# A hybrid decoder step: the recurrence entered out of the last attention step, its inputs read back in five batches, and the output norm and gate taken by thirds of the tokens over four row strips

## What is computed

```python
x = x + 0.5 * swiglu(rms_norm(x, ffn1_norm), ffn1_up, ffn1_down)
z_rw, q, k, v, gates = split(rms_norm(x, mix_norm) @ w_in)
y_a, wkv, z_new = rwkv7_branch(z_rw, z_last, wkv0)     # the recurrence
o = attend(rope(q), rope(k), v)                        # two softmax maps per head, p1 - lam * p2
y_b = rms_norm(o, da_subln) * (1.0 - lam_init)         # over the 128 values of each of 4 heads
merged = sigmoid(gates_a) * (y_a @ w_proj_a) + sigmoid(gates_b) * (y_b @ w_proj_b)
x = x + merged @ w_out
x = x + 0.5 * swiglu(rms_norm(x, ffn2_norm), ffn2_up, ffn2_down)
# the end of rwkv7_branch, y from the scan over the tokens, 8 heads of 64:
y = (y - mean(y)) * rsqrt(var(y) + RW_GN_EPS)
y = y * rw_ln_w + rw_ln_b + sum(r * k * rw_r_k) * v
y = y * g                                              # g = sigmoid(gd) @ rw_g2
```

## Time and profile before

| | us |
|---|---|
| time, median of 3 runs | 2895.99 (2893.55 to 2904.36) |
| profiled execution, its own time | 2896.66 |
| its span, first to last instruction | 2895.0 |
| PE busy in it | 2737.5 (95%) |
| DVE busy | 1376.1 (48%) |
| ACT busy | 655.8 (23%) |

### The profile page before, as it was taken

How to read it: one execution, slowest core, us unless ns; L and a number is a source line. 1 busy time by engine, 2 the same in 40 slices (tenths; PEclk the granted TensorE clock), 3 DMA queues, 4 the chain that set the end, 5 groups by cost and what they waited for, 6 DMA issues and landing times.

```text
span 2895.0 us, 51864 instructions
## 1 busy us (share of the span) xinstructions
PE 2737.5 (95%) x21419; PEld 2578.9 (89%) x21419; DVE 1376.1 (48%) x1452; ACT 655.8 (23%) x969; POOL 267.7 (9%) x258
## 2 busy tenths in 40 slices
PE   6999999999999999997777899899999999999998
PEld 6999999999999999995343789759999999999998
DVE  4332233223574688667663687655443322332333
ACT  5111111111311222332332233212222111110223
POOL 1000000000001233102000555200000000000000
PEclk8999999999999999997988899969999999999999
DMA  3111111111323455569645000124211111111112
GB/s 103 44 51 51 44 43 47 48 49 40 112 87 103 154 170 188 190 191 344 202 126 152 27 26 25 32 89 132 78 47 43 50 45 51 43 50 45 44 42 75
DMA packets 270206, 252.12 MB, mean 87 GB/s; under 512 B 20724, under 2 KB 216144, under 8 KB 269920
## 3 DMA queue, kind: packets, MB, share of 16 engines
q1 hardware_dynamic: 252960, 189.42, 21.9%
q0 software_dynamic: 16896, 60.40, 5.7%
q10 hardware_dynamic: 192, 0.07, 0.0%
HBM read 209.93 MB, written 39.90 MB: 86 GB/s over the span
## 4 chain that ended last, share of the span: by engine, by line
PE 87%; DVE 7%; ACT 2%; issue 1%; SPq 1%; DMA 1%; DVEq 0%; POOL 0%; POOLq 0%; ACTq 0%
PE ps L1746 72%; PE ps L2060 1%; DVE small L1469 1%; PE ps L2080 1%; PE ps L2075 1%; PE ps L1790 1%; PE ps L2263 1%; PE ps L1976 1%; PE ps L1910 1%; DMA value_ring<-in_cache_v 1%; PE ps L2107 1%; PE ps L1994 1%; PE ps L1953 1%; PE ps L2115 1%; PE ps L2087 1%
## 5 line engine op out<-in xcount | busy, mean ns | idle before, releaser
L1746 PE MATMUL ps<-h_hi,w_hi 128*128 128x344 f32 x3072 | 991.8, 323 | 10.3 <-DVE w_lo L1188 10.3
L1746 PE MATMUL ps<-h_lo,w_hi 128*128 128x344 f32 x3072 | 980.6, 319 | 0.0
L1746 PE MATMUL ps<-h_hi,w_lo 128*128 128x344 f32 x3072 | 980.1, 319 | 0.0
L1746 PEld LDWEIGHTS ps<-h_hi,w_hi 128*128 128x128 f32 x3072 | 577.7, 188 | 25.9 <-issue 19.8
L1746 PEld LDWEIGHTS ps<-h_lo,w_hi 128*128 128x128 f32 x3072 | 578.0, 188 | 2.1 <-issue 1.9
L1746 PEld LDWEIGHTS ps<-h_hi,w_lo 128*128 128x128 f32 x3072 | 577.9, 188 | 0.0
L1746 PE MATMUL ps<-ff_hi,w_hi 128*128 128x344 f32 x1056 | 337.1, 319 | 0.0
L1746 PE MATMUL ps<-ff_lo,w_hi 128*128 128x344 f32 x1056 | 336.6, 319 | 0.0
L1746 PE MATMUL ps<-ff_hi,w_lo 128*128 128x344 f32 x1056 | 336.2, 318 | 0.0
L831 ACT ACTIVATE w_hi<-w_stage 128x1024 fp32r<-128x1024 f32 x194 | 203.8, 1051 | 479.8 <-PE ps L1746 479.8
L1188 DVE TENSOR_TENSOR w_lo<-w_stage,w_hi 128x1024 fp32r<-128x1024 f32 x194 | 239.2, 1233 | 139.1 <-ACT w_hi L831 103.8
(11 more groups left out here) (402 smaller groups left out, 3233.7 us busy)
## 6 DMA issues: line engine op xcount, KB each, us to landing
w_stage<-in_ffn_up SPq DMA_DIRECT2D x176, 256.0 KB, 3.1
key_ring<-in_cache_k SPq DMA_DIRECT2D x128, 256.0 KB, 2.9
value_ring<-in_cache_v SPq DMA_DIRECT2D x128, 256.0 KB, 3.0
w_stage<-in_w_in SPq DMA_DIRECT2D x84, 256.0 KB, 3.3
w_stage<-in_ffn_down SPq DMA_DIRECT2D x80, 256.0 KB, 2.9
gate_save<-tmp POOLq DMA_DIRECT2D x16, 516.0 KB, 4.5
gate_ring<-gate_save POOLq DMA_DIRECT2D x16, 516.0 KB, 4.3
row_ring<-row_save SPq DMA_DIRECT2D x40, 128.0 KB, 2.9
```

Of the source, the lines that this page charges most:

```text
L1746: last = mm(dense[s][:, j], w[w0][:, k0 + k, :], r[:, k, j * CH:(j + 1) * CH], start=(k == 0 and n == 0), stop=(k == nk - 1 and n == 2))
```

## The change

It does six things.

1. The groups of cached values are used in steps 4 to 29 in place of 4 to 31; steps 17, 19, 22, 25, 26 and 28 take two.
2. POOL's queue reads the recurrence's inputs back in five batches of four DMAs, each behind a wait for scores 10, 13, 16, 19 and 22.
3. The squares for the head norm are taken from each step's 128x128 output in bank 6 by ACT, straight behind the copy into `Q`. PE sums them in the next step (`square_sum`, one output row at partition 32 * head). ACT copies four rows at a time into `rmix`, and DVE adds and inverts them block by block (`o_inverse`).
4. `decays(0)` moves into step 30 on ACT. POOL's `gram_sides(0)` waits for the last transposes but one and for the last value group, no longer for the head norm's sums. PE's `blocks(0)` follows the last output's copy and square.
5. In the first chunk DVE inverts 136 columns where it inverted 1032.
6. The output norm and gate run by thirds of the tokens (344 columns): each of 12 parts makes four matmuls, one per head, from rows 0, 32, 64 and 96 into four banks, and DVE works on the four heads of a third. The order is bonus, root, gate, then the head norm's scale.

The core of the diff (the table of semaphores, tile places and two memsets left out):

```diff
-        FILL_STEP = [s for s in range(HP, STEPS) for _ in range(2 if s >= STEPS - HP else 1)]
+        FILL_STEP = [s for s in range(HP, STEPS - 2) for _ in range(2 if s in (17, 19, 22, 25, 26, 28) else 1)]
...
-            for dst, src, done in ((KKn, kk_save, "kk_back"), (Bf, b_save, "b_back"), (Kf, kp_save, "kp_back"),
-                                   (Rf, r_save, "r_back"), (Vf, v_save, "v_back")):
+            for dst, src, done, step in ((KKn, kk_save, "kk_back", 10), (Bf, b_save, "b_back", 13), (Kf, kp_save, "kp_back", 16),
+                                         (Rf, r_save, "r_back", 19), (Vf, v_save, "v_back", 22)):
+                pool.wait_ge(*ev.at("scores_done", step))
...
-            pool.wait_ge(*ev.at("o_sums", 1))
+            pool.wait_ge(*ev.at("w_trans_lo", STEPS - 1))
+            pool.wait_ge(*ev.at("w_trans_hi", STEPS - 1 - 4 * HP))
+            pool.wait_ge(*ev.at("value_used", 4 * NS))
...
+                if step == STEPS - 2:
+                    act.wait_ge(*ev.at("cum_back0", 16))
+                    act.wait_ge(*ev.at("gate_saved0", 8 * GT))
+                    act.wait_ge(*ev.at("gate_saved1", 8 * GT))
+                    decays(0)
                 act.wait_ge(*ev.at("o_done", step + 1))
-                sc.activation(Q[:, step % HP, qi * P:(qi + 1) * P], PS[:, 6, 0:P], ACT.Copy)\
-                    .then_inc(ev["o_moved"], 1)
+                sc.activation(Q[:, step % HP, qi * P:(qi + 1) * P], PS[:, 6, 0:P], ACT.Copy)
+                if step and step % HP == 0:
+                    sc.activation(rmix[:, (qi - 1) * P:qi * P], PS[:, 6, P:2 * P], ACT.Copy, scale=1.0 / P).then_inc(ev["o_rows"], 1)
+                if step == STEPS - 1:
+                    sc.activation(rmix[0:96, qi * P:NP], PS[0:96, 6, P:2 * P], ACT.Copy, scale=1.0 / P)
+                sc.activation(osq, PS[:, 6, 0:P], ACT.Square).then_inc(ev["o_moved"], 1)
...
-            act.wait_ge(*ev.at("o_sample", NS))
-            for h in range(HP):
-                sc.activation(osq[:, h, :], Q[:, h, :], ACT.Square).then_inc(ev["o_sq"], 1)
-            act.wait_ge(*ev.at("o_mean", 1))
-            sc.activation(rmix[0:HP], rmix[0:HP], ACT.Sqrt).then_inc(ev["o_root"], 1)
-            act.wait_ge(*ev.at("cum_back0", 16))
-            act.wait_ge(*ev.at("gate_saved0", 8 * GT))
-            act.wait_ge(*ev.at("gate_saved1", 8 * GT))
...
+            act.wait_ge(*ev.at("o_sample", NS))
+            sc.activation(osq_sample, Q[:, :, NP:NT], ACT.Square).then_inc(ev["o_sq"], 1)
             decays(1)
+            act.wait_ge(*ev.at("o_sums", 1))
+            sc.activation(rmix[96:P, NP - P:NP], PS[96:P, 3, 0:P], ACT.Copy, scale=1.0 / P)
+            sc.activation(rmix[:, NP:NT], PS[:, 3, P:P + NS], ACT.Copy, scale=1.0 / P).then_inc(ev["o_rows"], 1)
...
+            def o_inverse(qi):
+
+                b = slice(qi * P, (qi + 1) * P if qi < 7 else NT)
+                dve.wait_ge(*ev.at("o_rows", qi + 1))
+                in_turn(v.tensor_scalar(rmix[:, b], rmix[:, b], 0.0, EPS, ALU.max, ALU.add))
+                in_turn(v.reciprocal(rmix[:, b], rmix[:, b]).then_inc(ev["o_inverse"], 1))
...
+                if qi and step % HP == 1:
+                    o_inverse(qi - 1)
...
-                    dve.wait_ge(*ev.at("o_root", 1))
-                    in_turn(v.reciprocal(rmix[0:HP], rmix[0:HP]).then_inc(ev["o_rstd"], 1))
+                    o_inverse(7)
...
+            def square_sum(step, bank, at):
+
+                row = 32 * (step % HP)
+                return mm(PS[row:row + 1, bank, at:at + P], K("ones")[:, 0:1], osq, start=True, stop=True)
...
+                    square_sum(step - 1, 6, P)
...
-            turn_sums(NS - 1)
-
-            pe.wait_ge(*ev.at("o_sample", NS))
-            for h in range(HP):
-                pe.wait_ge(*ev.at("o_sq", h + 1))
-                for j in range(NCH):
-                    last = mm(dense[0][0:HP, j], osel[:, HP * h:HP * h + HP], osq[:, h, j * CH:(j + 1) * CH],
-                              start=(h == 0), stop=(h == HP - 1))
-            last.then_inc(ev["o_sums"], 1)
-            pe.wait_ge(*ev.at("o_mean", 1))
...
+            pe.wait_ge(*ev.at("o_moved", STEPS))
             blocks(0)
+            square_sum(STEPS - 1, 3, 0)
+            pe.wait_ge(*ev.at("o_sq", 1))
+            for h in range(HP):
+                last = mm(PS[32 * h:32 * h + 1, 3, P:P + NS], K("ones")[:, 0:1], osq_sample[:, h, :], start=True, stop=True)
+            last.then_inc(ev["o_sums"], 1)
...
-                in_turn(v.scalar_tensor_tensor(ch3(y), ch3(y), param("rw_ln_w", h), dense[part % 2], ALU.mult, ALU.mult)
-                        .then_inc(ev["y_used"], 1))
-                dve.wait_ge(*ev.at("y_parts", part + 2))
-                in_turn(v.tensor_tensor(ch3(t1), ch3(Vf[:, h, :]), dense[(part + 1) % 2], ALU.mult).then_inc(ev["y_used"], 1))
-                in_turn(v.scalar_tensor_tensor(y, y, param("rw_ln_b", h), t1, ALU.add, ALU.add))
-                if h:
-                    ya_low(h - 1)
-                dve.wait_ge(*ev.at("y_parts", part + 3))
-                in_turn(v.tensor_tensor(ch3(y), ch3(y), dense[part % 2], ALU.mult).then_inc(ev["y_used"], 1))
...
+                b, bonus = third_of(j), spread_at(j)
+                in_turn(v.tensor_tensor(ybonus[:, :, b], Vf[:, :, b], bonus, ALU.mult).then_inc(ev["y_used"], 1))
+            for j in range(NCH):
+                b, root = third_of(j), spread_at(NCH + j)
+                for h in range(HP - 1):
+                    in_turn(v.scalar_tensor_tensor(CUM[:, h, b], CUM[:, h, b], param("rw_ln_w", h), root[:, h], ALU.mult, ALU.mult))
+                in_turn(v.scalar_tensor_tensor(CUM[:, HP - 1, b], CUM[:, HP - 1, b], param("rw_ln_w", HP - 1), root[:, HP - 1],
+                                               ALU.mult, ALU.mult).then_inc(ev["y_used"], 1))
+                in_turn(v.tensor_tensor(CUM[:, :, b], CUM[:, :, b], ybonus[:, :, b], ALU.add))
+            for j in range(NCH):
+                b, gate = third_of(j), spread_at(2 * NCH + j)
+                for h in range(HP - 1):
+                    in_turn(v.scalar_tensor_tensor(CUM[:, h, b], CUM[:, h, b], param("rw_ln_b", h), gate[:, h], ALU.add, ALU.mult))
+                in_turn(v.scalar_tensor_tensor(CUM[:, HP - 1, b], CUM[:, HP - 1, b], param("rw_ln_b", HP - 1), gate[:, HP - 1],
+                                               ALU.add, ALU.mult).then_inc(ev["y_used"], 1))
+                if j:
+                    ya_low(j - 1)
+            for j in range(NCH):
+                b, scale = third_of(j), spread_at(3 * NCH + j)
+                for h in range(HP - 1):
+                    in_turn(v.scalar_tensor_tensor(ybonus[:, h, b], Q[:, h, b], param("da_subln", h), scale[:, h], ALU.mult, ALU.mult))
+                in_turn(v.scalar_tensor_tensor(ybonus[:, HP - 1, b], Q[:, HP - 1, b], param("da_subln", HP - 1), scale[:, HP - 1],
+                                               ALU.mult, ALU.mult).then_inc(ev["yb_full"], 1))
+                if j == 0:
+                    ya_low(NCH - 1)
+                else:
+                    yb_low(j - 1)
+            yb_low(NCH - 1)
...
-            for part in range(3 * HP):
-                h, kind = divmod(part, 3)
-                if part >= 2:
+            pe.wait_ge(*ev.at("ck_rows_in", NC))
+            for part in range(4 * NCH):
+                kind, j = divmod(part, NCH)
+                first, b = part % 2 * HP, third_of(j)
+                if part == 1:
+                    pe.wait_ge(*ev.at("wkv_made", 1))
+                if 2 <= part < 3 * NCH + 2:
                     pe.wait_ge(*ev.at("y_used", part - 1))
-                if part == 0:
+                if part == NCH:
                     pe.wait_ge(*ev.at("y_root", 1))
-                if part == 2:
+                if part == 2 * NCH:
                     pe.wait_ge(*ev.at("g2_loaded", 16))
                     pe.wait_ge(*ev.at("gd_back", 16))
-                q = slice(32 * h, 32 * h + 2)
-                for j in range(NCH):
-                    cols = slice(j * CH, (j + 1) * CH)
-                    if kind < 2:
-                        last = mm(dense[part % 2][:, j], K("row_heads")[q], Rf[q, kind, cols], start=True, stop=True)
-                    else:
-                        last = mm(dense[part % 2][:, j], G2[:, h * P:(h + 1) * P], gd[:, cols], start=True, stop=True)
+                if part == 3 * NCH:
+                    pe.wait_ge(*ev.at("o_root", 1))
+                if part == 4 * NCH - 1:
+                    pe.wait_ge(*ev.at("yb_full", 1))
+                for h in range(HP):
+                    out, q = PS[:, first + h, 0:CH], slice(32 * h, 32 * h + 2)
+                    if kind == 0:
+                        last = mm(out, K("row_heads")[q], Rf[q, 1, b], start=True, stop=True)
+                    if kind == 1:
+                        last = mm(out, K("row_heads")[q], Rf[q, 0, b], start=True, stop=True)
+                    if kind == 2:
```

(3 more changed lines are left out.)

120 lines of the change are left out of this document (55 added, 65 removed).

## The result

The changed kernel takes 2882.72 us (median of 13 runs, 2874.29 to 2886.55), the kernel before 2895.99 beside it (13 runs, 2891.59 to 2904.36): a ratio of 0.994, with a 95% interval of 0.993 to 0.995. It is faster by 0.6%. 1.5% was forecast, and 2882.72 lies above the range of 2843 to 2867. The profiled execution is the fastest of the 13: own time 2874.29, span 2872.5. The 13 fall into two groups, six from 2874.29 to 2878.65 and seven from 2882.72 to 2886.55; only one of the lower group was profiled, so what the upper group pays in addition isn't shown.

A forecast was written before the change was run, and what follows sets the result against it. Prediction: PE bounds the kernel, held back at the attention's exit, first chunk, and norm and gate. 2896.66 - 28.4 - 5.5 - 14.2 + 5 = 2853.6 us, forecast as 2853.5 (-1.5% against the median), range 2843 to 2867.

The forecast's parts named there:

- term 4: Attention: added squares, doubled value groups and late reloads cost +6.5 us summed, taken as +5, bounds -2 to +15.
- Late reloads: Attention, in term 4: three batches fall in waiting steps, each late by perhaps 1.2 us; first groups save 1: +2.5.
- each batch costs what its DMAs take in steps that wait, 3 x 5: Attention, upper bound of term 4: +15 us, with the rest cancelling.
- Later ones have most of a step in hand: Attention, in term 4: steps from 16 on have slack for late groups, so only three batches cost time.
- The clock: Attention, in term 4: PE's clock level was allowed 1 us each way.
- Term 1: Recurrence's start: `blocks(0)` can start 3.1 us after the last output's start in place of 31.6, gain 28.4 us.
- Term 2: First chunk: DVE's 6.59 us inversion becomes an addition and inversion of 136 columns, gain 5.5 us, between 3.5 and 7.
- Term 3: Norm and gate: four strips run side by side, DVE becomes the bound at 42.6 us; gain 14.2 us, bounds 11 to 16.
- Term 4 without the reloads: Attention: squares, doubled groups, `o_inverse` and shorter late steps, the +5 or +6.5 us less 2.5 for reloads.
- the attention pays much more: Rival, attention: batches stretch groups in flight, doubled steps run out of pages, 13 us plus 3 for squares; 2865 to 2874, chance 0.16.
- the stretches that were put at nothing: Before the first output product, the recurrence after its first chunk, and merge to the end: forecast difference 0.

The follow-up runs named there:

- early_again: The changed kernel with its twenty reload transfers issued together ahead of the attention, measured a second time: 2859.00 us, ratio 0.9869 to the kernel before.
- before_late: The kernel before with only the reloads changed, to five batches behind scores 10, 13, 16, 19 and 22: 2914.46 us, ratio 1.0053.
- before_later: The kernel before with the reloads in five batches behind scores 19, 21, 23, 25 and 27: 2897.70 us, ratio 0.9998.
- last_two_late: The changed kernel with three reload batches issued ahead of the attention, only the last two late, behind scores 19 and 22: 2866.85 us, ratio 0.9882.
- norm_by_head: The changed kernel with reloads ahead of the attention and the two norms and gate computed head by head as before: 2870.57 us, ratio 0.9905.
- early_reloads: The changed kernel with its twenty reload transfers issued together ahead of the attention, as before: 2855.29 us, ratio 0.9846 to the kernel before.
- two_queues: The changed kernel with reloads ahead of the attention and two of each value group's four pages issued by POOL's queue: 2856.36 us, ratio 0.9851.
- two_queues_first: As two_queues, but POOL issues its pages of the first two value groups ahead of the twenty reloads: 2853.98 us, ratio 0.9863.

## Why the prediction was wrong

The step that failed is in term 4, "Late reloads": each batch is 5.4 us "during which a group lands a little later", three batches fall in steps that wait, "each late by perhaps 1.2", in sum +2.5. The profiled executions show 246.7 - 223.0 = 23.7 us (19.9 against `early_again`), the medians 27 and 24. Two things in that step were wrong, and a third was left out.

- **The size of one.** A batch doesn't delay a group by a part of its 5.4 us but by 4 to 7 us, about all of it. By the trace a group whose load meets a batch is back 10.7 to 13.6 us after its half is free (15.6 for one in a doubled step), in place of 7. The upper bound in the same term, "each batch costs what its DMAs take in steps that wait, 3 x 5", is what `before_late` measured, 15.4. The argument for the small number was that SP's issue takes longer than the landing and that the DMA share is 0.27 in a late stretch. Both are true and neither bears on it: in the kernel before, groups 2 to 11 are wanted 5 to 10 us after their half is free and are back after 7 to 10, so most of a delay of 4 us or more is waited for. The 2.06 MB of a batch count a KB as 1000 bytes; at 1024 it is 2.11 MB and 5.5 us, which changes nothing here.
- **The number of them.** "Later ones have most of a step in hand" holds for one group a step, and `before_later` shows that they do. The change doubles groups in steps 17, 19 and 22 itself, which takes that slack away, and `last_two_late` puts some 10 us on the two batches there (11.6 by the medians, 10.3 to 14.1 by the attention). That 15.4 and 11.6 add up to just 27 is in part luck, given the scatter. I priced the two edits apart, each against the kernel before. Their cost is in the pair.
- **The clock.** Term 4 has 1 us each way for it. With the late reloads PE's products in the attention take 6.5 us longer, at a mean clock of 0.85 in place of 0.89 (2.9 longer against `early_again`, at 0.88).

The other terms, as forecast and measured:

- **Term 1**, 28.4 and 27.1. POOL and ACT were on time. The last output at the lower clock, 3.78 us in place of 2.02, is what was missing.
- **Term 2**, 5.5 and 5.2.
- **Term 3**, 14.2 and 13.4, or 15.6 counted from the copy of the state (1873.86 to 1918.89, before 1879.92 to 1940.57), and 15.3 by `norm_by_head`. Strips side by side and DVE as the bound were both right; the gate parts were not late. The Trainium skill's page "TensorEngine Tiling (Array Packing)", section "Theoretical Speedup", agrees here with its up to four times: 0.86 us for four products where one is estimated at 0.6, so 2.8 times, and 3.2 times at the lower clock (1.53 us where one takes 1.21).
- **Term 4 without the reloads**, +5 less the 2.5 for them, and +3.7 measured with `early_reloads`, +7.5 with `early_again`. What the squares cost is not clear of zero. The steps 17, 19, 22, 25 and 26 are 1.5, -0.2, 3.1, -0.2 and 3.4 us longer than before, 7.6 in place of 4, most of it in step 26 behind the doubled step 25 and in step 22, which ran at a clock of 0.70 here and is 0.9 us longer than before where the clock is full. The prediction had step 26 as covered by PE's wait for ACT and left out that its pages come late. The four steps 27 to 30 take 39.6 us in place of 44.6: 5 back in place of 3.

Of the rivals, "the attention pays much more" was the case: its mechanism (batches that stretch every group in flight, and doubled steps that run out of pages) was right, but its price of 13 + 3 us was again too small for 22 more than forecast. That sum took 13 us as waited for; PE's idle time grew by 17, and the lower clock came on top. The miss of the profiled execution against 2853.6 is 20.7 us: +22.4 from the attention, +1.3, +0.3 and +0.8 from the terms 1 to 3, and -4.2 from the stretches that were put at nothing. The other 8.4 us up to the median of 2882.72 is this kernel's scatter, of which the profiled execution had the low end; where they lie is open. With the reloads early the ratio is 0.9846 and 0.9869, and the forecast 0.9853: but for this one step the time came out. That it did so this closely is in part luck, since the misses of the terms 1 to 3 are offset by the 4.2 us of the stretches that were put at nothing.

## What to carry to other kernels

Here twenty transfers cost 21 to 27 us more in five batches beside a ring of two buffers than in a stretch in which hardly a buffer was wanted. A batch in a step without slack cost about its whole time at full bandwidth, some 5 us; where the time from "buffer free" to "buffer wanted" had room for it, it cost nothing measurable. Compare these two times, not the mean DMA share. And where one change both adds traffic and uses up the slack of the same ring, price the two together.

## What the runs showed of the hardware

- While the last output product runs, the granted clock is at its lower level of 1.2 GHz in the changed kernel, and was at the upper one, 2.4 GHz, before. The windows of PE alone (us, busy, granted clock, DMA share, GB/s), before:

```profile
1566.00:1569.00 3.00, 2.02 (x16) 1.00 0.81 251
```

  After, with the transposes ahead of it, which PE began behind 4.51 idle us; in the kernel before, value groups stand in that place. `early_reloads` has the same 4.51 idle us and the lower level too:

```profile
1588.48 1.97 PE L2038 MATMUL ps<-const,probs 128*128 128x128 f32 x8 [4.51 <-DVE probs L1504]
```

```profile
1592.00:1595.50 3.50, 3.50 (x16) 0.50 0.20 14
```

- Pages on POOL's queue landed 20.2 us after their issue behind twenty reloads of 516 KB (`two_queues`), where SP's land in 3.0 in the median. SP's pages beside the end of the same burst in `two_queues_first` took 6.9: what is queued behind a burst waits for the burst, what stands in another queue for a part of it.

```profile
value_ring<-in_cache_v SPq DMA_DIRECT2D x4, 256.0 KB, 6.9
```

- Products of 1 or 2 rows in four row strips overlap for the most part: 0.86 us at the upper clock level and 1.53 at the lower one for four of 344 columns, where one in a strip by itself takes 1.21 at the lower one.
